# Expert scores of a decoder step: high and low rows of h side by side as 512 moving columns from the 48th U tile on

## The reference

```python
eidx, g = ...                 # per token 8 heads x 16 experts and their softmax weights
a = gelu(einsum('td,ted->te', x, expert_u[eidx]))
y = einsum('te,ted->td', g * a, expert_v[eidx])
```

## Time and profile before

| | |
|---|---|
| median of 3 runs | 1054.61 us (1050.43 to 1058.03) |
| the profiled execution | 1056.62 us, its span 1055.0 us |
| mean granted TensorE clock | 0.995 |
| busy share | PE 98%, PE weight loads 84%, DVE 70%, ACT 41%, POOL 42% |
| U stage with gates (n = 48 to 111) | 382.3 to 628.8 us |
| U tiles 112 to 127 | 628.8 to 675.0 us |

### The profile page before, as it was taken

One profiled execution on the slowest core, in us unless ns is written; L12 is line 12 of the kernel. 1 busy time (PEld: TensorE's weight loads), 2 busy tenths in 40 slices (PEclk: granted clock), 3 DMA queues, 4 the chain that ended last, 5 costly groups with the idle time before them and its releaser, 6 DMA issues.

```text
span 1055.0 us, 19777 instructions
## 1 busy us (share of the span) xinstructions
PE 1033.3 (98%) x6961; PEld 888.2 (84%) x6961; DVE 734.7 (70%) x1486; ACT 431.1 (41%) x747; POOL 447.9 (42%) x329
## 2 busy tenths in 40 slices
PE   6999999999999998999999999999999999999998
PEld 3447778889999998999999999878788887888776
DVE  2549999649999738888888885655455555555554
ACT  2123322343456453343434344544444444444442
POOL 4753333245687876777777771011111111111110
PEclk8999999999999999999999999999999999999999
DMA  9425468358755567888888876676667666676663
GB/s 338 122 88 176 143 207 339 107 201 297 255 181 185 179 231 261 273 281 264 288 278 275 275 236 222 215 267 218 200 227 252 219 226 220 242 243 226 221 219 106
DMA packets 79438, 237.40 MB, mean 225 GB/s; under 512 B 11749, under 2 KB 23661, under 8 KB 78980
## 3 DMA queue, kind: packets, MB, share of 16 engines
q1 hardware_dynamic: 65052, 195.51, 55.1%
q0 software_dynamic: 13040, 40.52, 11.4%
q10 hardware_dynamic: 1280, 0.53, 0.2%
HBM read 233.56 MB, written 3.14 MB: 224 GB/s over the span
## 4 chain that ended last, share of the span: by engine, by line
PE 85%; DVE 9%; DMA 3%; issue 1%; POOL 1%; ACT 1%; ACTq 0%; SPq 0%; DVEq 0%
PE psum L980 33%; PE psum L1045 32%; PE psum L991 5%; PE psum L574 4%; DVE top L1585 3%; DVE work_s L1586 2%; PE psum L810 2%; PE psum L1076 2%; PE psum L783 1%; DMA w_raw<-expert_v 1%; DMA w_raw<-expert_ut 1%; POOL w_lo L1489 1%; PE psum L558 1%; PE psum L590 1%; PE psum L932 1%
## 5 line engine op out<-in xcount | busy, mean ns | idle before, releaser
L1489 POOL TENSOR_TENSOR w_lo<-w_raw,w_hi 128x1024 fp32r<-128x1024 f32 x116 | 281.2, 2429 | 107.4 <-ACT w_hi L1097 106.2
L1097 ACT ACTIVATE w_hi<-w_raw 128x1024 fp32r<-128x1024 f32 x214 | 226.7, 1059 | 211.9 <-PE psum L1045 103.9
L980 PE MATMUL psum<-h_hi,w_hi 128*128 128x256 f32 x1024 | 297.1, 290 | 0.2 <-issue 0.2
L980 PE MATMUL psum<-h_lo,w_hi 128*128 128x256 f32 x1024 | 290.2, 283 | 0.0
L980 PE MATMUL psum<-h_hi,w_lo 128*128 128x256 f32 x1024 | 290.1, 283 | 0.0
L980 PEld LDWEIGHTS psum<-h_hi,w_hi 128*128 128x128 f32 x1024 | 196.8, 192 | 1.9 <-issue 1.6
L980 PEld LDWEIGHTS psum<-h_lo,w_hi 128*128 128x128 f32 x1024 | 197.0, 192 | 0.0
L980 PEld LDWEIGHTS psum<-h_hi,w_lo 128*128 128x128 f32 x1024 | 196.7, 192 | 0.0
L1517 POOL DMA_INDIRECT rows_in<-expert_v,eidx x32 | 44.1, 1379 | 326.3 <-PE psum L1076 321.3
L1826 DVE TENSOR_TENSOR w_lo<-w_raw,w_hi 128x1024 fp32r<-128x1024 f32 x98 | 120.1, 1225 | 77.8 <-ACT w_hi L1097 77.8
L1045 PE MATMUL psum<-w_hi,ag_hi 128*128 128x512 f32 x512 | 160.4, 394 | 2.1 <-DVE ag_lo L1833 2.1
(11 more groups left out here) (286 smaller groups left out, 1383.3 us busy)
## 6 DMA issues: line engine op xcount, KB each, us to landing
w_raw<-expert_ut SPq DMA_DIRECT2D x128, 512.0 KB, 4.9
w_raw<-expert_v SPq DMA_DIRECT2D x86, 512.0 KB, 4.1
raw_more<-expert_v SPq DMA_DIRECT2D x42, 512.0 KB, 4.3
w_slice<-w_pq_cols SPq DMA_DIRECT2D x32, 512.0 KB, 5.4
rows_in<-h_save SPq DMA_DIRECT2D x32, 512.0 KB
w_most<-w_in_blocks SPq DMA_DIRECT2D x8, 699.0 KB, 12.6
w_slice<-w_o_half SPq DMA_DIRECT2D x8, 512.0 KB, 4.7
v_cache<-cache_v POOLq DMA_DIRECT2D x64, 64.0 KB, 3.5
```

The costliest lines, as they stand in the source:

```text
L980: mm = pe.matmul(psum[:, 2 + s, 0:SEQ], a[:, s, c, :], b[:, c, :], start=(i == 0), stop=(i == 3 * KC - 1))
L1097: return act.activation(out, in_, ACT.Copy)
L1489: pool.tensor_tensor(w_lo[:, s], w_raw[:, s], w_hi[:, s].bitcast(F32), ALU.subtract).then_inc(S["w_lo_ready"], 1)
```

## The change

For n >= 48 the matmuls of w_hi with h_hi and h_lo become one matmul with 512 moving columns, which fills the whole PSUM bank: the high part's product in columns 0 to 255, the low part's in 256 to 511. The w_lo product still goes to columns 0 to 255. So a tile has 8 matmuls of 512 columns and 8 of 256. The two halves have to be added before the gelu: ACT copies columns 256 to 511 to `u_low` in SBUF, and DVE adds them onto columns 0 to 255 (`add_low`). The product of the one-hot eq with the weight moves from DVE (one instruction of 512 columns) to ACT (`hot_i`, four instructions of 128 columns with a scale per partition). Tiles below 48 have the same 24 matmuls on the new layout.

```diff
-    h_hi = take("h_hi", [P, KC, SEQ], F32R)
-    h_lo = take("h_lo", [P, KC, SEQ], F32R)
+    h_split = take("h_split", [P, KC, 2, SEQ], F32R)
+    u_low = take("u_low", [P, 2, SEQ])
...
-                i = 0
+                out = psum[:, 2 + s, 0:SEQ]
                 for c in range(KC):
-                    for a, b in ((w_hi, h_hi), (w_hi, h_lo), (w_lo, h_hi)):
-                        mm = pe.matmul(psum[:, 2 + s, 0:SEQ], a[:, s, c, :], b[:, c, :],
-                                       start=(i == 0), stop=(i == 3 * KC - 1))
-                        i += 1
+                    if wide:
+                        pe.matmul(psum[:, 2 + s, :], w_hi[:, s, c, :], h_split[:, c].rearrange("p a t -> p (a t)"),
+                                  start=(c == 0), stop=False, skip_group_check=True)
+                    else:
+                        for a in range(2):
+                            pe.matmul(out, w_hi[:, s, c, :], h_split[:, c, a], start=(c == 0 and a == 0), stop=False)
+                    mm = pe.matmul(out, w_lo[:, s, c, :], h_split[:, c, 0], start=False, stop=(c == KC - 1),
+                                   skip_group_check=wide)
                 mm.then_inc(S["prod_done"], 1)
...
+            def hot_i(k):
+
+                act.wait_ge(S["eq_ready"], k + 1)
+                if k >= 2:
+                    act.wait_ge(S["g_psum"], k - 1)
+                for b in range(NB):
+                    t = NB * k + b
+                    a = act.activation(i_hot[:, k % 2, b, :], eq_ps[:, b, :], ACT.Copy, scale=wT[:, t:t + 1])
+                a.then_inc(S["i_hot_ready"], 1)
+
             def gated(m, s, done=SEQ, ends=False):
                 n = RING * m + s
                 act.wait_ge(S["prod_done"], n + 1)
+                copy(u_low[:, s % 2, :], psum[:, 2 + s, SEQ:2 * SEQ]).then_inc(S["u_low_ready"], 1)
+                act.wait_ge(S["u_summed"], n - (G_AT - 1))
                 a = act.activation(psum[:, 2 + s, 0:done], psum[:, 2 + s, 0:done], ACT.Gelu)
...
+            hot_i(0)
             for k in range(G_STEPS):
+                if k + 1 < G_STEPS:
+                    hot_i(k + 1)
                 gated((G_AT + k) // RING, k % RING, weighed(k))
...
                 if k:
-                    dve.wait_ge(S["hot_ready"], k)
+                    dve.wait_ge(S["i_hot_ready"], k)
+                dve.tensor_tensor(eq_ps, bc(iota_ps, 1, NB), bc(iT[:, token], 2, NU), ALU.is_equal
+                                  ).then_inc(S["eq_ready"], 1)
                 if k >= 2:
                     dve.wait_ge(S["g_psum"], k - 1)
-                dve.tensor_tensor(eq_ps, bc(iota_ps, 1, NB), bc(iT[:, token], 2, NU), ALU.is_equal
-                                  ).then_inc(S["eq_ready"], 1)
-                dve.tensor_tensor(j_hot[:, k % 2], bc(iota_ps, 1, NB), bc(jT[:, token], 2, P), ALU.is_equal)
-                dve.wait_ge(S["eq_ready"], k + 1)
-                dve.tensor_tensor(i_hot[:, k % 2], eq_ps, bc(wT[:, token], 2, NU), ALU.mult
-                                  ).then_inc(S["hot_ready"], 1)
+                dve.tensor_tensor(j_hot[:, k % 2], bc(iota_ps, 1, NB), bc(jT[:, token], 2, P), ALU.is_equal
+                                  ).then_inc(S["j_hot_ready"], 1)
+
+            def add_low(n):
+
+                s = n % RING
+                dve.wait_ge(S["u_low_ready"], n - (G_AT - 1))
+                dve.tensor_tensor(psum[:, 2 + s, 0:SEQ], psum[:, 2 + s, 0:SEQ], u_low[:, s % 2, :], ALU.add
+                                  ).then_inc(S["u_summed"], 1)
...
                 if n in DOT_AT:
                     dot(DOT_AT.index(n))
+                add_low(n)
                 weigh(k)
             for n in range(G_END - 1, NU):
                 gate(n % RING, n, G_STEPS)
...
                 if n + 3 >= LO_FROM:
                     low_w(n + 3)
+                if n + 1 < NU:
+                    add_low(n + 1)
```

More of the change, by code:

```diff
@@ L967, in low_in, with prod_u @@
                     pe.wait_ge(S["w_lo_dve"], n - LO_FROM + 1)
-            def prod_u(s, n, free=True, late=False):
+            def prod_u(s, n, free=True, late=False, wide=True):
                 pe.wait_ge(S["w_hi_ready"], n + 1)
@@ L976, in prod_u @@
                     pe.wait_ge(S["act_free"], n - 3)
-                i = 0
+                out = psum[:, 2 + s, 0:SEQ]
                 for c in range(KC):
-                    for a, b in ((w_hi, h_hi), (w_hi, h_lo), (w_lo, h_hi)):
-                        mm = pe.matmul(psum[:, 2 + s, 0:SEQ], a[:, s, c, :], b[:, c, :],
-                                       start=(i == 0), stop=(i == 3 * KC - 1))
-                        i += 1
+                    if wide:
[6 more added lines that the diff above has]
+                                   skip_group_check=wide)
                 mm.then_inc(S["prod_done"], 1)
             def spread(s, k, free=True):
-                pe.wait_ge(S["hot_ready"], k + 1)
+                pe.wait_ge(S["j_hot_ready"], k + 1)
+                pe.wait_ge(S["i_hot_ready"], k + 1)
                 if free:
@@ L998, in _ @@
                     pe.wait_ge(S["rs_copied"], 4)
-                prod_u(n % RING, n, n >= RING)
+                prod_u(n % RING, n, n >= RING, wide=False)
                 if n < 12 and n % 3 == 1:
@@ L1009, in _ @@
                 for s in range(RING):
-                    prod_u(s, RING * m + s)
+                    prod_u(s, RING * m + s, wide=False)
             for t in range(3):
@@ L1260, in _ @@
             act.wait_ge(S["h2_ready"], KC)
-            copy(h_hi[:], h2[:, :, 0:SEQ]).then_inc(S["h_hi_p"], 1)
+            copy(h_split[:, :, 0, :], h2[:, :, 0:SEQ]).then_inc(S["h_hi_p"], 1)
             copy_q(2)
@@ L1484, in _ @@
             pool.wait_ge(S["pnew_ready"], 2)
-            pool.tensor_tensor(h_lo[:], h2[:, :, 0:SEQ], h_hi[:].bitcast(F32), ALU.subtract).then_inc(S["h_lo_p"], 1)
+            pool.tensor_tensor(h_split[:, :, 1, :], h2[:, :, 0:SEQ], h_split[:, :, 0, :].bitcast(F32),
+                               ALU.subtract).then_inc(S["h_lo_p"], 1)
             def low_w(s, n):
```

## The result

The changed kernel takes 1101.88 us (median of 6 runs, 1099.73 to 1104.65) against 1055.42 for the kernel before: a ratio of 1.045, 95% interval 1.042 to 1.048, slower by 46 us. The profiled execution took 1099.73 us, its span is 1098.0 against 1055.0. The forecast was 1099 for the profiled execution, 1097 to 1099 against the median, with a range of 1084 to 1116.

The account below looks back on a forecast made before the run. TensorE bounded the kernel before; after the change a loop over VectorE, ScalarE and POOL would set the pace. The loop's +41 us and 2 for the last tiles gave 1056.6 + 43 = 1099 us, range 1084 to 1116.

Parts of the forecast that it names:

- The ring: Tiles 49 to 111: dot, add_low, gelu, split, low_w, fetch, low_w, next dot; 9.02 us per two tiles against PE's 7.33.
- three order links: Queue orders in the loop: add_low behind the dot, split behind the gelu that waits for add_low, dot behind low_w.
- hop of 0.05: Hand-over from VectorE's add_low to ScalarE, estimated at about 0.05 us from POOL's 0.08 start after a split.
- The tail: U stage after the last dot: tile 114 starts 5.5 us later, then 14 x 2.77 = 38.8 us, plus 2 lost.
- the sum: Whole kernel: 41 us more up to the U stage's end and 2 for the last tiles, 1056.6 + 43 = 1099 us.
- the second ring: Tiles 113 to 127: add_low, gelu, split, VectorE's low_w, 3.03 us per tile against PE's 2.77; may lose 0 to 4.
- ScalarE's branch: ScalarE's way from the dot through hot_i, copy and gelu to split(n + 4), ending at 5.9 us with 0.6 slack.
- the rival: ScalarE's products cost 0.4 us or more each, or the hand-overs do, giving 1110 to 1120 us; chance 12%.
- the 11 us more: At 0.41 us per part of hot_i, ScalarE's way would be about 0.35 us late per pair, some 11 us in all.
- the shape of TensorE's idle time: Gate steps: PE idle 1.7 us in each pair of tiles, waiting for POOL's w_lo.
- the clock's rival: PE's 1.7 us gaps lower TensorE's clock; with a further 0.5 us per pair the time is 1115 us; chance 7%.
- The PE-bound rival: Gate steps: the loop does not decide, PE keeps 3.66 us per step, 8.5 us are saved, time 1048 us; chance 10%.

Follow-up runs that it names:

- e2: Changed kernel with ScalarE's split of tile n + 3 put ahead of its wait for add_low: 1058.91 us, ratio 1.007 to the kernel before.
- e3: Changed kernel with VectorE's add_low(n) put ahead of dot(n): 1083.13 us, ratio 1.029 to the kernel before.
- e4: Changed kernel with dot(n) waiting only for low_w(n) instead of low_w(n + 2): 1093.99 us, ratio 1.040 to the kernel before.
- e8: Changed kernel with i_hot made by VectorE again: 1099.63 us in two runs, ratio 1.042 to the kernel before.
- e7: Changed kernel with i_hot on VectorE again and ScalarE's split ahead of its wait for add_low: 1045.31 us, ratio 0.992 to the kernel before.

## Why the prediction was right

**The mechanism.** The ring was forecast at 9.02 us per pair and is 8.99 (535.42 to 544.41), 8.98 in the mean of 31. Its three order links are shown one by one: cut at ScalarE 7.75 (e2), moved at VectorE 8.35 (e3), and the third, the dot behind low_w, is made by the hardware too (e4).

**Term by term.** Dot to add_low 1.15, as forecast; add_low to gelu 0.46 (0.47 forecast); gelu to split 0.34 (0.33); split to low_w 1.13 (1.14); low_w to the dot 5.91 (5.93). All but the hop of 0.05, an estimate, were read from the trace of before, as a distance from start to start or as the duration of an instruction whose successor waits for its end. That they fit says that the hand-overs cost as much in the new order.

**The tail.** Tile 114 starts at 675.38, 5.48 after the last dot, as the sum has it. From there to the end of U it is 41.0 us where I had 38.8: the second ring with 2.97 us per tile (689.61, 692.58, 695.55 for three tiles' starts; 3.03 forecast) binds from tile 119 on, and V waits 2.58 for ag_lo instead of 0.77. Together this cost 4.0 where the sum had 2. The ring alone did not do it: it was set back once by a late tile load, which the sum did not have in the tail. These are VectorE's low_w of tiles 118 and 119 and ScalarE's split of 119:

```profile
683.65 1.23 DVE L1852 TENSOR_TENSOR w_lo<-w_raw,w_hi 128x1024 fp32r<-128x1024 f32 x1 [0.54 <-ACT w_hi L1102]
688.29 1.23 DVE L1852 TENSOR_TENSOR w_lo<-w_raw,w_hi 128x1024 fp32r<-128x1024 f32 x1 [2.21 <-ACT w_hi L1102]
```

```profile
687.19 1.06 ACT L1102 ACTIVATE w_hi<-w_raw 128x1024 fp32r<-128x1024 f32 x1 [1.57 <-DMA w_raw<-expert_ut]
```

The load was on the chain of waits from 681.20 on and took 5.97 us, against a median of 4.4. The two low_w are 4.64 apart instead of 2.97, so up to 1.67 of the 4.0 is its part; that is an estimate, and no run tests it. The large ring cost 1.8 less than the sum (669.9 for the last dot, 671.7 forecast). The two misses cancel, and that is luck: the profiled execution came out within 1 us of the forecast by it. By the medians the change is 46.5 us, not 43, so 1101.88 lies 3 above the 1097 to 1099 that the prediction gave for the median.

**ScalarE's branch.** hot_i's products start 0.25 apart and last 0.38, between the bounds of 0.16 and 0.31 by the copies for the spacing. The split of tile 83 ends at 532.62 and POOL takes it up at 532.98: 0.36 us of slack where the prediction had 0.6, so the rival did not come true. e8, without these products, has the same 8.98 per pair. The 0.41 per product by the Trainium skill's page "ScalarE: Activation LUTs" (section "Rules for kernel authors", row on a tight latency budget) is near the duration of one; the cost in a queue is 0.25, and the 11 us more that went with it did not come.

**One step failed**, the shape of TensorE's idle time. I had one gap of 1.7 us per pair, for POOL's w_lo. There are two: 0.64 to 0.86 before a spread (for i_hot or j_hot) and 0.25 to 0.42 before a tile's first wide matmul (for w_lo), together 18.4 us in the 148, or 1.1 per pair as the profile counts idle time (1.6 by the starts: 8.98 less twice 3.68, the step at 532.10 to 535.78), since TensorE reaches the spread before its one-hots are made. It changed nothing in the sum, TensorE having room. The clock stayed at 1.00 in the steady part, so the clock's rival did not come true, but its premise, a gap of 1.7 us, was never met there: the steady part does not test it.

**The PE-bound rival** had the right time for another kernel: e7's ratio of 0.992 would make 1048.6 of 1056.6, against 1048 forecast, with one order changed and i_hot put back.

## What to carry to other kernels

Before a wait is added to a queue, list what stands behind it in that queue and ask whether the instruction waited for stands, in its own queue, behind something that this work feeds. If so the durations add up around a ring, however idle the engines are. Issue what feeds others (here the split) ahead of the new wait: that one order was worth 43 us, four to five times what the wide matmuls could gain. Then look again, since the next shorter ring may be closed by another part of the change (here i_hot on ScalarE).

## What the runs showed that was not expected

VectorE's dot (two SBUF inputs) beside POOL's subtraction takes 3.30 instead of 1.23 us, while the subtraction, which had started first, kept 2.39 (e4). The other way round it is the subtraction that gets longer: in e2 one that starts at 524.50, while the dot of 523.76 runs, takes 2.75 instead of 2.40. So in these traces the one that starts second loses about the time for which the other still runs. And the length of an idle time does not alone decide TensorE's clock. In the changed kernel TensorE was idle 2.39 us before 675.38, and the granted clock stayed 1.00 in the stretches around and after it, whereas the kernel before fell to 0.50 after 1.88 us:

```profile
675.38 0.47 PE L980 MATMUL psum<-h_split,w_hi 128*128 128x512 f32 x1 [2.39 <-ACT w_hi L1102]
```

```profile
672.00:678.00 6.00, 3.61 (x21) 2.97 (x20) 3.07 (x7) 4.18 (x8) 4.93 (x3) 1.00 0.35 119
678.00:684.00 6.00, 6.00 (x36) 5.27 (x35) 3.91 (x7) 3.46 (x7) 2.47 (x2) 1.00 0.71 221
```

Before V it was idle 2.58 us (until 718.94), and the clock stayed 1.00 there too. What decides it no run here shows.
